# Two recurrence levels back to back, and the projection products of two slots together, in a hybrid decoder kernel

## The reference

```python
x = x + 0.5 * swiglu(rms_norm(x), w_gate, w_up, w_down)
(nq, ck, cv, sk, sv, wk, wv, ng, dq, dk, dv, hq, hf, hi, hg) = split_cols(rms_norm(x) @ w_in)
# NSA: 6 heads; differential attention: 4 heads; both need q and k normed per head
# HGRN2: 6 heads of 64, gated linear recurrence over the 512 tokens:
scores[t, s] = sum_k q[t, k] * k[s, k] * exp(cum[t, k] - cum[s, k])      # s <= t
o_h = scores @ v
x = x + concat(o_nsa, o_diff, o_h) @ w_out
```

## Time and profile before

| | |
|---|---|
| time, median of 3 runs | 2242.29 us (2241.99 to 2242.84) |
| profiled execution: its own time, and its span | 2242.77 us, 2240.9 us |
| TensorE busy | 99% of the span |
| VectorE, ScalarE, GpSimd busy | 53%, 41%, 7% |
| recurrence of layer 0 | 447.5 to 550.1 us |
| recurrence of layer 1 | 1559.4 to 1661.3 us |

### The profile page before, as it was taken

How to read it: one execution, slowest core, us unless ns; L and a number is a source line. 1 busy time by engine, 2 the same in 40 slices (tenths; PEclk the granted TensorE clock), 3 DMA queues, 4 the chain that set the end, 5 groups by cost and what they waited for, 6 DMA issues and landing times. The chain is left out here.

```text
span 2240.9 us, 29162 instructions
## 1 busy us (share of the span) xinstructions
PE 2219.2 (99%) x11564; PEld 1754.8 (78%) x11564; DVE 1185.0 (53%) x1933; ACT 916.6 (41%) x1517; POOL 156.3 (7%) x157
## 2 busy tenths in 40 slices
PE   9999999999999999999999999999999999999999
PEld 6888888876657888888888888878766578888887
DVE  6444433577775444433664443346776764444336
ACT  5222223545784322223552232235557743222234
POOL 0000000033111000000000000000431210000000
PEclk9999999999999999999999999999999999999999
DMA  5422334312113233333223333343121133233332
GB/s 195 136 95 95 96 94 142 131 59 76 55 31 95 94 103 95 98 106 100 94 95 94 98 100 90 100 149 117 57 82 41 43 97 98 94 102 100 96 99 84
DMA packets 69125, 214.41 MB, mean 96 GB/s; under 512 B 8158, under 2 KB 15326, under 8 KB 68990
## 3 DMA queue, kind: packets, MB, share of 16 engines
q1 hardware_dynamic: 60260, 191.09, 27.3%
q10 hardware_dynamic: 8650, 21.37, 2.9%
q0 software_dynamic: 80, 0.09, 0.0%
HBM read 208.30 MB, written 5.40 MB: 95 GB/s over the span
## 5 line engine op out<-in xcount | busy, mean ns | idle before, releaser
L529 PE MATMUL main<-xh,wh 128*128 128x512 f32 x1896 | 754.1, 398 | 1.7 <-ACT vv L1242 1.1
L530 PE MATMUL main<-xl,wh 128*128 128x512 f32 x1896 | 739.5, 390 | 0.0
L531 PE MATMUL main<-xh,wl 128*128 128x512 f32 x1896 | 739.2, 390 | 0.0
L1553 DVE TENSOR_TENSOR wl<-raw,wh 128x1024 fp32r<-128x1024 f32 (+2 forms) x337 | 405.5, 1204 | 356.2 <-ACT wh L1035 354.9
L1035 ACT ACTIVATE wh<-raw 128x1024 fp32r<-128x1024 f32 (+3 forms) x371 | 376.5, 1016 | 459.2 <-PE main L531 425.9
L529 PEld LDWEIGHTS main<-xh,wh 128*128 128x128 f32 x1896 | 356.3, 188 | 100.4 <-issue 22.9
L531 PEld LDWEIGHTS main<-xh,wl 128*128 128x128 f32 x1896 | 356.3, 188 | 75.4
L530 PEld LDWEIGHTS main<-xl,wh 128*128 128x128 f32 x1896 | 356.6, 188 | 74.4 <-issue 3.4
L529 PE MATMUL main<-ffh,wh 128*128 128x512 f32 x704 | 273.9, 389 | 0.0
L530 PE MATMUL main<-ffl,wh 128*128 128x512 f32 x704 | 273.9, 389 | 0.0
L531 PE MATMUL main<-ffh,wl 128*128 128x512 f32 x704 | 273.9, 389 | 0.0
(11 more groups left out here) (264 smaller groups left out, 2082.1 us busy)
## 6 DMA issues: line engine op xcount, KB each, us to landing
raw<-in_ffn_up SPq DMA_DIRECT2D x88, 512.0 KB, 3.5
raw<-in_ffn_gate SPq DMA_DIRECT2D x87, 512.0 KB, 3.5
raw<-in_ffn_down SPq DMA_DIRECT2D x64, 448.0 KB, 3.3
raw<-in_w_in_t SPq DMA_DIRECT2D x40, 512.0 KB, 3.5
raw<-in_ffn_down SPq DMA_DIRECT2D x32, 512.0 KB, 3.5
raw<-in_wout SPq DMA_DIRECT2D x24, 384.0 KB, 3.2
w<-in_cmp_w ACTq DMA_DIRECT2D x16, 512.0 KB, 4.2
raw<-in_ple_gate SPq DMA_DIRECT2D x16, 512.0 KB, 3.3
```

The source lines that it names most:

```text
L529: nc.tensor.matmul(out, lh, rh, start=start, stop=False, **kw)
L530: nc.tensor.matmul(out, lh, rl, start=False, stop=False, **kw)
L531: return nc.tensor.matmul(out, ll, rh, start=False, stop=stop, **kw)
L1553: nc.vector.tensor_tensor(wl[:, c % SLOTS, 0:n], raw[:, c % SLOTS, 0:n], wh[:, c % SLOTS, 0:n], ALU.subtract).then_inc(*tick("weights_lo", ...
```

## The change

TensorE's loop now goes over two slots at a time: the values of the pair of heads that is through first, then both levels, then the products of both slots, then the head sums, then the compressed scores. So both levels of two slots stand on the four side banks at once. The slots in which a tile is scaled and squared (`tiles_scaled`) and its head factor and norm are made (`tiles_factored`) are even ones now, at the start of the next two slots and of those after it. On ScalarE the copies of the natural-order projection (`natural_values`) are before the far scores in slot 8. Everything else on VectorE, ScalarE and GpSimd keeps its order.

```diff
+def tiles_scaled(slot):
+    return [name for name in GROUP_OF["A"][:-1] if LAST_PART[name] // 2 * 2 + 2 == slot]
+def tiles_factored(slot):
+    return [name for name in GROUP_OF["A"][:-1] if min(LAST_PART[name] // 2 * 2 + 4, 3 * (LEVELS + 1) - 1) == slot]
...
                 def hgrn():
-                    for slot in range(3 * (LEVELS + 1)):
+                    for slot in range(0, 3 * (LEVELS + 1), 2):
                         p, lev = slot // (LEVELS + 1), slot % (LEVELS + 1) - 1
-                        level(p, lev)
                         if p and lev < 0:
                             hgrn_values(p - 1)
-                        if p and lev == 0:
+                        level(p, lev)
+                        level(p, lev + 1)
+                        for s in (slot, slot + 1):
+                            if s < NAT_SLOTS:
+                                natural_half(s // 2, s % 2)
+                            for name, ks in PARTS.get(s, {}).items():
+                                tile_part(name, ks)
+                        if p and lev < 0:
                             head_squares(("hgrn", p - 1), "sum64")
-                        if slot < NAT_SLOTS:
-                            natural_half(slot // 2, slot % 2)
-                        for name, ks in PARTS.get(slot, {}).items():
-                            tile_part(name, ks)
-                        for name in tiles_after(slot, 2):
+                        for name in tiles_scaled(slot):
                             head_squares(name, "sum32" if name[0] == "d" else "sum64")
-                        if (p, lev) == (2, 2):
+                        if (p, lev) == (2, 1):
                             compressed_scores()
...
# ScalarE
-                            for name in tiles_after(slot, 3):
+                            for name in tiles_factored(slot):
                                 head_factor(name, DIFF_QK if name[0] == "d" else HEAD)
+                            if slot == NAT_SLOTS:
+                                natural_values((0, 1))
                             if lev >= 7:
                                 far_scores(p, lev)
...
-                            if slot in (NAT_SLOTS, NAT_SLOTS + 1):
-                                natural_values(((0, 1), (2, 3))[slot - NAT_SLOTS])
+                            if slot == NAT_SLOTS + 1:
+                                natural_values((2, 3))
...
-                            for name in tiles_after(slot, 1):
+                            for name in tiles_scaled(slot):
                                 act.wait_ge(*done("scaled", name))
                                 head_square(name, zt(name))
...
# VectorE
-                            for name in tiles_after(slot, 1):
+                            for name in tiles_scaled(slot):
                                 scaled(name, zt(name))
...
-                            for name in tiles_after(slot, 3):
+                            for name in tiles_factored(slot):
                                 normed(name)
```

More of the change, by code:

```diff
@@ L100 @@
 PARTS, LAST_PART = slot_parts()
-def tiles_after(slot, distance):
-    return [name for name in GROUP_OF["A"][:-1] if LAST_PART[name] + distance == slot]
+def tiles_scaled(slot):
+    return [name for name in GROUP_OF["A"][:-1] if LAST_PART[name] // 2 * 2 + 2 == slot]
+def tiles_factored(slot):
+    return [name for name in GROUP_OF["A"][:-1] if min(LAST_PART[name] // 2 * 2 + 4, 3 * (LEVELS + 1) - 1) == slot]
 MAPS = NSA_HEADS + DIFF_HEADS
```

## The result

The changed kernel takes 2258.79 us in the median of 5 runs (2257.7 to 2262.06); the kernel before takes 2242.54 beside it. The ratio is 1.0077, 95% interval 1.0066 to 1.0089. The forecast was 2253, range 2241 to 2264.

What follows compares the result with a forecast made beforehand. TensorE, busy 2219.2 of 2240.9 us, was taken as the bound. Added waits less 6.1 us saved per layer gave 5.9 us longer in layer 0 and 4.7 in layer 1, together 10.6: 2253 us, range 2241 to 2264.

Steps and rivals of the forecast that it cites:

- The gain: TensorE in the recurrence: pairing levels saves switches, and two kinds of main-bank wait go, 6.1 us saved per layer.
- level 15: Tile nq0, second level of a pair: waits 2.6 us for the head sum's bank, freed by ScalarE's late logarithm.
- level 23: Head sum of hgrn 1, second level of a pair: waits 1.75 us for the bank the logarithm frees.
- level 27: Tile wk, second level of a pair: waits 2.0 us, with compressed scores and sk's norm in VectorE's queue.
- levels 13, 19, 21: Second levels after a head sum where nothing else is late: each waits 0.35 us, 1.2 us in all.
- hgrn_values, two: Values of heads, now first: wait for ScalarE's far scores, 0.65 us at hgrn_values(0) and 1.0 at hgrn_values(1).
- end, layer 0: Attention's first scores wait for all of level 29's far copies, behind dk0's head factor: 2.65 us instead of 0.66.
- end, layer 1: Attention's first scores wait for the logarithm only, as the bank turn is shifted by three: 0.8 us instead of nothing.
- rival 4: Clock falls: after long waits products run at 1.2 GHz, 3.4 us more each, six make 20, 2273 us; chance 0.04.
- Rival 1: VectorE has slack, logarithms come before the second levels, only gains stay: 12.9 us faster, 2229.4 us; chance 0.13.
- rival 3: A pair of levels costs as much as two alone: waits stay, 9.4 us of gain gone, 2262 us; chance 0.06.
- Rival 2: Half the waits: chains to second levels 2 us shorter each, about 5 us a layer goes, 2243 us; chance 0.12.

Runs made afterwards that it cites:

- e3: Kernel before, with only the levels and products of slots 0 to 7 taken in pairs on TensorE, where no head sum falls: 2237.51 us.
- e1: Changed kernel, with head sums moved off the side banks to main bank 3 and values of heads to main 2: 2247.49 us.
- e2: Changed kernel, with ScalarE's head factors (the logarithm) put before the decay of their slot, same banks: 2250.33 us.
- e7: Changed kernel without the pairing: each level again in front of its own slot's products, all other engines and head sums as changed: 2251.84 us.
- e4: Changed kernel, with the far scores of level 29 before the head factor of dk0 on ScalarE: 2253.33 us.
- e5: Changed kernel, with head sums on main bank 3 (values of heads on main 1), values after both levels, level 29's far scores before dk0's head factor: 2241.02 us.
- e6: Kernel of e5, with VectorE's weight splits of the tiles one slot later: 2238.94 us.
- e8: Kernel of e3, with ScalarE's natural-order values before far scores in slot 8 and level 29's far scores before dk0's head factor: 2238.03 us.
- e9: Kernel of e3, with levels 18 and 19, and 28 and 29, also paired: 2240.61 us.
- e10: Kernel of e9, with the two ScalarE orders of e8, and head sums on main bank 3 (values of heads on main 1): 2235.47 us.

## Why the prediction was right, point by point

**The gain.** 6.1 us a layer were forecast. A pair of levels takes 1.09 us to its product (1.10 forecast), and e3 shows 0.38 for a pair against 0.36. Both rows of waits for main banks went. The whole gain can only be had by subtraction: the waits in the table below, less what the stages grew by without the half clock (5.5 and 5.7 us) and, in layer 0, the old wait of 0.66, leave 7.0 us in both layers. So it was 0.9 larger than forecast. A part of that is level 15's old wait of 0.25 us, which the sum counted in the new 2.6 and never took off; the first pair (0.85) and 0.02 more for each of 13 pairs give another 0.3; the rest stays open.

**The waits at second levels.** Right in place and cause, and in size within 0.35 us each. They come to 10.5 us a layer without the end, 10.0 were forecast. In the table, each is the distance of starts less what the same step takes without a wait, in layer 1 of the changed kernel, except that level 15 and the end of layer 0 are read in layer 0:

| | forecast | measured |
|---|---|---|
| level 15 | 2.6 | 2.6 |
| level 23 | 1.75 | 2.1 |
| level 27 | 2.0 | 1.8 |
| levels 13, 19, 21 | 1.2 | 1.3 |
| levels 25, 26, sum of wk | 0.8 | 0.9 |
| hgrn_values, two | 1.65 | 1.8 |
| end, layer 0 | 2.65 | 2.7 |
| end, layer 1 | 0.8 | 2.2 |

e1, e2 and e7 shorten the waits of levels in three ways: another bank, an earlier logarithm, products in between. Who waits for what was read right against the profile's word: it puts level 15 down to sdiag in both kernels, and e2, which leaves VectorE's order alone, removes that wait. That level 15 came out to the hundredth is partly luck: levels 23 and 27, reckoned in the same way, are 0.35 and 0.2 off.

**The end in layer 1** is a term mis-sized, 0.8 against 2.2. I let the attention's scores start on side banks 0 and 1 in both layers, as the description of the kernel says; that holds for layer 0 alone. Their turn over five banks goes on from layer 0: 121 takes there, so layer 1 starts one bank further and meets level 29's bank. e4 took 2.1 us away there. That the forecast still came near without the clock is partly chance: 1.4 us too little here and 0.5 a layer in the other waits stand against 0.9 a layer too little in the gain.

**The clock** was rival 4, given 0.04, and it came on top of my forecast. Without it the stages are 5.5 and 5.7 us longer, 11.2 in all, where 10.6 was forecast. Three stretches at half clock, two in the stage and one behind it, cost about 1.6 us each: 15 products took 5.23 us in slots 14 and 15 of layer 0 and 3.65 in layer 1, from rows like these of the changed kernel, layer 0 and then layer 1:

```profile
497.88 0.63 PE L536 MATMUL main<-xh,wl 128*128 128x512 f32 x1
498.30 0.63 PE L534 MATMUL main<-xh,wh 128*128 128x512 f32 x1
...
1619.71 0.40 PE L535 MATMUL main<-xl,wh 128*128 128x512 f32 x1
1619.95 0.40 PE L536 MATMUL main<-xh,wl 128*128 128x512 f32 x1
```

That is 4.7 us, as much as the profiled span (15.3 us longer) passed the 10.6 that were forecast; the 0.6 us of the stages is offset by a start of the first stage 0.7 us earlier. The median of five grew by 16.3, and how many stretches the other four executions had is not shown. I had priced 3.4 us for each of six; measured were half of that, and three: in the first, matmuls start 0.42 us apart (497.88 to 498.30), against 0.24 in layer 1 (1619.71 to 1619.95), but for about eight of the 15 products only. The step that failed is the sentence that gave this case 0.04 and kept it apart from the main one: it needs the long waits that I forecast, so it was no alternative to them. By the Trainium skill, TensorE: Matmul & The Clock Gate, section Part 1: The HAM clock gate, an idle TensorE goes back to half clock. The trace agrees in layer 0, with 0.50 behind waits of 2.41, 1.84 and 2.53 us; layer 1 waited 2.41, 1.84 and 2.08 us at the same places and stayed at 1.00.

**The other rivals.** Rival 1 (waits hidden) and rival 3 (no gain) are out: the waits are there, and e3 has the gain. Rival 2 needed chains 2 us shorter; level 15's is 9.17 us before and 9.15 after.

## What to carry to other kernels

When work is grouped to save switches, ask of each bank or buffer in turn who frees it and what that engine does first; the products that lay between two users were its cover. A chain already at its limit in the trace of before (here a logarithm ending 0.14 us ahead of a level) will show in full once the cover is moved. Group where no third user takes from the same banks: e3 alone gave 2237.5 us. Giving such a user a bank of its own was part of the best kernel, 2235.5 us, together with two changes of order.

## What the runs showed of the hardware

Long waits can cost TensorE twice. In all kernels together the stages have 16 waits of 1.8 us or more (up to 2.6). Behind 8 of them the clock was 0.50 for a stretch that began between 0.1 us before and 1.5 us after the end of the wait: three in the changed kernel, one each in e1, e2 and e7, two in e4. The length of the wait does not decide it: 1.84 us in layer 0 of the changed kernel had one and 2.41 in layer 1 none; in e2 2.08 had one and 2.53 none. The changed kernel's five runs spread over 4.4 us, those of before over 0.9 in the five beside it and 2.4 in twenty others; that the stretches make the difference fits, but was not tried. None of e3, e5, e6, e8, e9, e10 had one in a stage, with waits up to 1.8 us.

Where a product of GpSimd and a weight split of VectorE overlap, one of the two takes longer; alone they take about 0.73 and 1.22 us. In the kernel before, a split that started 0.02 us ahead of a product took 1.95 us and the product 0.85; in e1, at the same place and the same distance, the split took 1.23 and the product 1.92. A product that started 0.2 to 0.5 us ahead of a split kept its 0.72 to 0.75 us, and the split took 1.3 to 1.6. In e6 the second of the two products shown above started 0.28 us into the split and took 1.71 us alone. Beside a keep the pair took 1.44. Why they delay each other no run here tries apart.
